# A hybrid decoder trunk: weight stream in parts of 1024 columns through two raw buffers, in place of 512 through four

## What is computed

```
h = rms_norm(x, attn_pre_g[l]);  u = h @ w_in[l]              # 1024 x 2560
y = concat(conv_mixer(u), retention(u), moba_attention(u), pool_mixer(u))
x = x + rms_norm(y @ w_out[l], attn_post_g[l])                # 1024 x 1024
h = rms_norm(x, ffn_pre_g[l])
f = (silu(h @ w_gate[l]) * (h @ w_up[l])) @ w_down[l]         # d_ff = 2816
x = x + rms_norm(f, ffn_post_g[l])
```

## Time and profile before

| | |
|---|---|
| median of 3 runs | 1225.34 us (1222.08 to 1226.42) |
| the profiled execution | 1229.54 us, its span 1227.7 us |
| granted TensorE clock, mean | 0.968 |
| PE busy | 1136.5 us, 93% of the span |
| DVE busy, ACT busy | 654.0 us (53%), 451.5 us (37%) |
| weight transfers | 376 of 256 KB, median 3.2 us from issue to landing |
| read from HBM | 102.43 MB, 85 GB/s over the span |

### The profile page before, as it was taken

The page is one execution under the profiler, slowest core; times in us unless marked ns, Lnnn a source line. Parts: engine busy times, 40 slices in busy tenths (PEclk is TensorE's granted clock), DMA queues, the critical chain, the costliest instruction groups (busy, mean ns, idle before and its releaser), DMA issues. The chain is left out here.

```text
span 1227.7 us, 20295 instructions
## 1 busy us (share of the span) xinstructions
PE 1136.5 (93%) x8328; PEld 840.8 (68%) x8328; DVE 654.0 (53%) x1522; ACT 451.5 (37%) x944; POOL 5.0 (0%) x22
## 2 busy tenths in 40 slices
PE   7787988998999999999996899999799999999996
PEld 6676866887744444888895787678685444468895
DVE  6768885676533333320858788747764333332033
ACT  7414453554433333221523335455453322231022
POOL 1000000000000000000000000000000000000000
PEclk9989998998999999999998899889999999999998
DMA  7522121113633323330312231100343333332001
GB/s 272 163 69 84 55 70 35 35 36 106 204 103 99 100 99 102 104 100 19 104 43 96 70 104 36 58 24 23 104 144 131 104 103 103 104 103 69 1 14 57
DMA packets 57181, 105.85 MB, mean 86 GB/s; under 512 B 6912, under 2 KB 7296, under 8 KB 56960
## 3 DMA queue, kind: packets, MB, share of 16 engines
q1 hardware_dynamic: 57088, 104.55, 26.4%
HBM read 102.43 MB, written 2.10 MB: 85 GB/s over the span
## 5 line engine op out<-in xcount | busy, mean ns | idle before, releaser
L509 PE MATMUL bank<-hT,ring 128*128 128x256 f16 (+1 forms) x3456 | 557.9, 323 | 7.9 <-DVE hT L1291 5.1
L509 PEld LDWEIGHTS bank<-hT,ring 128*128 128x128 f16 x3456 | 339.8, 99 | 219.1 <-issue 6.6
L509 PE MATMUL bank<-U,ring 128*128 128x256 f16 x2880 | 325.0, 274 | 0.3
L509 PEld LDWEIGHTS bank<-U,ring 128*128 128x128 f16 x2880 | 283.1, 99 | 36.3 <-DVE E L1527 0.8
L1224 DVE SCALAR_TENSOR_TENSOR ring<-raw,ring 128x512 f16<-128x512 f32 x376 | 236.7, 686 | 108.5 <-ACT ring L829 107.1
L829 ACT ACTIVATE ring<-raw 128x512 f16<-128x512 f32 x376 | 209.5, 622 | 137.3 <-PE bank L509 101.6
L1527 DVE SCALAR_TENSOR_TENSOR E<-bank,E 128x512 f32<-128x512 f32 (+1 forms) x56 | 32.1, 577 | 243.1 <-ACT E L1021 242.7
L509 PE MATMUL bank<-ring,hT 128*128 128x256 f16 x1152 | 135.3, 277 | 0.0
L1021 ACT ACTIVATE E<-bank 128x512 f32<-128x512 f32 (+1 forms) x56 | 28.0, 503 | 263.2 <-PE bank L509 263.2
L509 PEld LDWEIGHTS bank<-ring,hT 128*128 128x128 f16 x1152 | 114.2, 100 | 15.3 <-DVE ring L1224 0.3
L1329 DVE SCALAR_TENSOR_TENSOR E<-E,parx 128x256 f32<-128x256 f32 x240 | 101.3, 478 | 0.1
(11 more groups left out here) (100 smaller groups left out, 550.1 us busy)
## 6 DMA issues: line engine op xcount, KB each, us to landing
raw<-weights_dram SPq DMA_DIRECT2D x376, 256.0 KB, 3.2
yT<-x_dram SPq DMA_DIRECT2D x4, 512.0 KB, 5.0
out_dram<-hT SPq DMA_DIRECT2D x8, 256.0 KB, 2.2
cst<-consts_dram SPq DMA_DIRECT2D x1, 1296.5 KB, 7.9
cst<-consts_dram SPq DMA_DIRECT2D x1, 128.0 KB, 4.3
bd<-pool_w_dram SPq DMA_DIRECT2D x8, 16.0 KB, 4.8
par<-params_dram SPq DMA_DIRECT2D x1, 108.0 KB, 4.1
cst<-consts_dram SPq DMA_DIRECT2D x1, 64.0 KB, 1.9
```

Source lines behind the costliest of these rows:

```text
L509: ins = mm(dst, st, mv_, start=first and i == 0, stop=last and i == 2, **kw)
```

## The change

Parts of 1024 columns in place of 512 and two raw buffers in place of four. `raw` still holds 1 MB. Every slot is loaded by 2 transfers of 512 KB (128 rows of 4096 B) in place of 4 of 256 KB (128 rows of 2048 B), and each split is 2 instructions on ACT and 2 on DVE with 1024 columns in place of 4 with 512. All other work, and the order of all steps, is unchanged; the conditions `n == PARTS - 1` and `n == 2 * PARTS - 1` in SP's loop put the second half of x behind the first slot and the constants behind the second, as before.

```diff
 SLOT = 2048
-PARTS = 4
+PARTS = 2
 RAW = SLOT // PARTS
-NRAW = 4
+NRAW = 2
 RING = 8
```

## The result

The changed kernel takes **1241.36 us** in the median of 4 runs (1236.23 to 1246.57), the kernel before 1225.88 beside it on the same chip (4 runs, 1222.08 to 1228.25). The ratio is 1.0129, 95% interval 1.0075 to 1.0184: slower by 1.3%. The forecast was 1230.5, with a range from 1226 to 1238.

What follows compares the result with a forecast made beforehand. PE, busy 93% of the span, bounds the kernel, except where it waits for DVE and ACT at start, mixers and turns. Terms 2.3 + 0.7 + 1.4 + 0.6 - 0.3 + 0.5 = 5.2 us on 1225.34 gave 1230.5, range 1226.0 to 1238.0.

Steps and rivals of the forecast that it cites:

- terms 1 to 4: Start (slots 0 to 4, 5 to 7), both feed-forward turns, layer 1's start: slower buffer rounds cost 2.3, 0.7, 1.4, 0.6 us.
- terms 5 to 8: Mixers -0.3 us, gate/up in half units 0, full units and down 0, clock +0.5.
- Slots 0 to 4, +2.3: Kernel start: rounds of 5.75 us instead of 4.2 make slot 4's last lo pass end 2.3 us later.
- rival A: Bursts: 512 KB lands in 4.4 us, not 3.4, second part queues behind first; terms 1 to 4 become 12, time 1238; chance 0.19.
- Slots 5 to 7, +0.7: Start, up to slot 7's end on DVE: 0.7 us later, bounds -1 and +2.
- The turns, +0.7 each: Turn to the feed-forward part, both layers: slot 20's lo ends later, 0.7 us each, bounds +0.1 and +1.8.
- Layer 1's start, +0.6: Slots 52 and 53: longer buffer rounds end slot 53's lo 0.6 us later, bounds 0 and +1.6.
- The mixers, -0.3: Both layers' mixers: splits waiting for ACT's first part lose 0.28 us, others win 0.13 or 0.17; -0.15 per layer.
- rival D: Whole kernel: first terms absorbed by later PE waits, mixers' wins cancel the rest, no effect, 1224 to 1228 us; chance 0.16.
- Half units, 0: Gate/up in half units: ACT falls 2.5 us behind, covered because PE needs the bank three units later; 0 us.
- Rival C: Gate/up half units: the cover fails, ACT's lag delays the silu freeing a bank; forecast + 5, 1236 us; chance 0.06.
- The clock, +0.5: After PE's long waits: longer waits may bring more half-clock time, +0.5 us, between 0 and +4.

Runs made afterwards that it cites:

- e7: The changed kernel with the parameters loaded before x, as SP's second transfer: 1236.82 us, 1.0073 of the kernel before.
- e15: One more trace of the changed kernel, no edit: 1247.44 us, mean granted clock 0.954.
- e3: The changed kernel with four more buffers of 1024 columns for slots 0 to 7: 1222.81 us, 0.9977 of the kernel before.
- e5: The kernel before with eight more buffers of 512 columns for the first 8 slots: 1216.98 us, 0.9908 of the kernel before.
- e6: The changed kernel with a third buffer of 1024 columns for slots 20 to 52 and 67 to 93: 1236.49 us, 1.0052 of the kernel before.
- e4: The changed kernel with 280 extra matmuls put ahead of PE's waits, results overwritten: 1235.08 us, 1.0083 of the kernel before.
- e8: The kernel before with the same 280 extra matmuls ahead of PE's waits: 1224.28 us, 0.9964 of the kernel before.
- e10: The changed kernel with the edits of e3, e6 and e7 together, parts of 1024: 1213.93 us, 0.9899 of the kernel before.
- e11: The kernel before with extra buffers at start and turns and parameters loaded second, parts of 512: 1215.97 us, 0.9896 of the kernel before.

## Why the prediction was wrong

The forecast had the mechanism and its sign, and the time is outside the range. **The step that failed is the size of terms 1 to 4**: the forecast put 5.0 us on the four places where buffers come round too slowly, and PE's list shows 9.9. The rest of the loss, 5.7 us where terms 5 to 8 had +0.2, has no shown cause. By the forecast's own steps:

1. **Slots 0 to 4, +2.3.** Slot 4's lo ends at 38.89 + 1.22 = 40.11 against 35.77: +4.3. The round was right (5.76). What was not in the walk is that the second part of a pair lands later than one DVE step after the first: it was taken as 1.15 us behind, and came 2.2 to 2.4 behind. At slot 2 the second transfer, issued 1.1 us after the first, took 4.6 us against 3.2, and the gap stayed in the rounds that followed. The part of rival A that said "the second part of a pair queues behind the first" was right, in a stretch for which the earlier trace rows seemed to exclude it. The first norm was also held by POOL for 1.3 us, but e7 took this wait away and the rotation stayed where it was.
2. **Slots 5 to 7, +0.7.** Slot 7's lo ends at 61.03 + 1.23 = 62.26 against 57.13, so +5.1 in all where terms 1 and 2 gave 3.0; this term came out at +0.8.
3. **The turns, +0.7 each.** This is a mis-sized term, too: +1.6 and +1.5 on PE. DVE after the change:

```profile
282.60 1.22 DVE L1224 SCALAR_TENSOR_TENSOR ring<-raw,ring 128x1024 f16<-128x1024 f32 x1 [3.25 <-ACT ring L829]
285.04 1.22 DVE L1224 SCALAR_TENSOR_TENSOR ring<-raw,ring 128x1024 f16<-128x1024 f32 x1 [1.22 <-ACT ring L829]
```

   From slot 19's hi (275.91) to the end of slot 20's lo (286.26) are 10.35 us; before, 275.38 to 283.90, 8.52. That is +1.8, and again the second part, 2.44 behind the first. It is the upper bound that the term gave. The second transfer took 4.6 us here as well.
4. **Layer 1's start, +0.6.** From slot 52's lo to slot 53's end 8.71 us (641.03 to 649.74) in place of 7.63: +1.1, inside the bounds; on PE +1.3 in the mean.
5. **The mixers, -0.3.** Slot 8's lo ends 3.45 us after its hi starts (73.18 to 76.63): 3.46 was forecast, 3.16 before. The price is right. The term can't be judged: the lateness fell from 5.1 us at the rotation to 0.7 at the norm in the first profile, 4.4 given back where the bound was 3; in e15 it rose, from 5.9 to 9.5 (PE's norm row at 244.09). The clock in the mixers moves them by more than the passes do. PE's idle time in layer 0's mixers did fall, from 21.2 us to 18.4 to 18.6 in all four traces, so the absorption that rival D named is there, but not enough to cancel the start.
6. **Half units, 0.** Right. ACT does fall behind (slot 27's lo ends at 341.4, before at 333.9), and PE shows no wait there. Rival C is out. **Full units, 0**: right.
7. **The clock, +0.5, with bounds of 0 and +4.** Not shown to be right or wrong. Outside the four places the traces have +2.0 us in all, where terms 5 to 8 had +0.2: +0.8 and +0.9 in the feed-forward parts, the rest in the mixers. Executions of the changed kernel differ by 13.5 us, the longest at the lowest clock, and the forecast read one profile of the kernel before. That the four us between its profiled execution and its median meant a spread was not taken into the range.

The sum of the account, in us: 9.9 at the four places, 2.0 elsewhere in the traces, and 3.7 by which the profiled execution of the kernel before was longer than its median make 15.6; the medians differ by 15.5. Only the first figure has its cause shown, and 8.6 of its 9.9: more buffers take away the start (e3 against e5, 7 us by the ratios) and the turns (e6), and e4 against e8 show both at full clock. No run took away the 1.3 of layer 1's start alone. Had terms 1 to 4 been sized right, the forecast would have been 1235.4, inside its own range; the time lies outside it by the other 5.7. Rival A, with 12 us for terms 1 to 4 and 1238 for the time, was the nearest. That the first profile came near the sum (6.7 against 5.2) was luck: its places cost as much as in the other traces, and short mixers hid it. The Trainium skill, page "DMA: Bandwidth & Descriptors", section "Rules for kernel authors", asks for larger transfers to reach the bandwidth; the measurement decides against it for this kernel: 512 KB in place of 256, with the passes that go with it, is slower where the buffers are short, and not measurably different where they are not (e10 against e11).

**What stays open.** Whether the longer waits bring more half-clock time later on, which would then be part of the missing 5.7 us, is not shown: e4 and e8 filled the waits and left the difference of the two kernels where it was. That e7 gains 7 us by the ratio with 0.5 us seen is the same riddle. Why the half-clock stretches of 190 to 230 and 780 to 830 us come in some executions and not in others was not found. No second trace of the kernel before was taken, so how much of the 3.7 us lies in its mixers is not known. A variant with more than 1 MB in `raw` for the whole run was not tried, nor was one with three buffers of 512 (a slot has four parts).

## What to carry to other kernels

With fixed bytes in a staging buffer, fewer and larger parts lengthen the loop landing, first pass, second pass, next issue (4.2 to 5.75 us here), because nothing of a part overlaps with itself; look for the stretches in which slots come faster than buffers, and lend them memory that is idle there (1% under the kernel before here, with parts of either size). Where a round's parts are issued in close order, price the second landing apart from the first (4.3 to 4.6 us here against 3.2). Work saved on engines that are a third to a half busy is worth nothing (29 us of it here). Where the granted clock changes from one execution to the next, compare several traces of both kernels from one fixed row of the list to the next before pricing a wait, and give the clock a range as wide as the differences between executions. Growth of PE's busy time is no price by itself, since it can take the place of waiting.

## What was not expected of the hardware

- A transfer of 512 KB landed in 3.4 us in the median, one of 256 KB in 3.2; the shortest were 3.1 and 2.4. So a landing depends little on the size in this stream. Of two transfers of 512 KB issued 1.2 us apart the second took 4.3 to 4.6 us and the first 3.2; issued 2.3 us apart, both took 3.1 to 3.2. The Trainium skill, page "DMA: Bandwidth & Descriptors", section "Anatomy of one DMA — SWDGE (gpsimd) path", gives for GpSimd's path about 2.0 us and bytes / 436e3, by which, as an estimate, 256 KB would take 2.6 and 512 KB 3.2 us; these transfers, issued by SP, come near it at their shortest, and their medians lie above.
- The same program took from 1235.0 to 1248.5 us, the kernel before 1224.1 to 1231.3, with the mean granted clock at 0.953 to 0.966 and 0.958 to 0.972. Traces of the changed kernel show it as PE busy 1136.1 to 1149.2 us for 8328 matmuls; most of the difference lies in the mixers, and the way through a turn differs by 0.4 us at most.
- 280 extra matmuls in PE's waits raised the mean clock from 0.962 to 0.978 and from 0.965 to 0.980 (each against runs of the same chip), and made either kernel 0.4% shorter.
